# A two-block transformer on one core: smaller gate pieces, a regrouped linear-attention branch, and turned branches evicted by another engine

## The reference

```
x = layer_norm(a*x + 0.5*swiglu(x, w1[0], w3[0], w2[0]))
mix = token_mixing(x)
x = layer_norm(a*x + mix)
x = layer_norm(a*x + 0.5*swiglu(x, w1[1], w3[1], w2[1]))
x = layer_norm(a*x + sigmoid(x @ ple_w_gate) * (p @ ple_w_proj))
```

```
h_rw, h_gla, h_gdn, h_gate = split(x @ w_in)
branches = stack(rwkv7(h_rw), gla(h_gla), gated_deltanet(h_gdn))   # 3 x 256 x 512
merged = sum(sigmoid(h_gate) * (branches @ w_branch))              # 3 x 256 x 1024, summed
return merged @ w_o
```

```
o = att @ v_c + (q_c * exp(b_c)) @ S
S = S * exp(b_end) + (k_c * exp(b_end - b_c)).T @ v_c
return rms_norm(o, norm_g) * silu(gate)
```

## Time and profile before

| | |
|---|---|
| median of 3 runs | 3145.26 us (3143.68 to 3149.9) |
| the profiled execution | 3148.42 us, its span 3146.6 us |
| TensorE busy | 2995.2 us (95%) |
| VectorE, ScalarE, GpSimd busy | 1777.4 us (56%), 694.2 us (22%), 43.8 us (1%) |
| mean granted TensorE clock | 0.986 of full speed |
| HBM read | 425.71 MB, 136 GB/s over the span |

### The profile page before, as it was taken

How to read it: one execution, slowest core, us unless ns; L and a number is a source line. 1 busy time by engine, 2 the same in 40 slices (tenths; PEclk the granted TensorE clock), 3 DMA queues, 4 the chain that set the end, 5 groups by cost and what they waited for, 6 DMA issues and landing times. The chain is left out here.

```text
span 3146.6 us, 52837 instructions
## 1 busy us (share of the span) xinstructions
PE 2995.2 (95%) x22782; PEld 2365.6 (75%) x22782; DVE 1777.4 (56%) x2647; ACT 694.2 (22%) x1326; POOL 43.8 (1%) x83
## 2 busy tenths in 40 slices
PE   8999998999999999999889999989999999998998
PEld 8987764559976998675467995655888887765897
DVE  5554555556556564454565565584433664486665
ACT  2102113212112101212312113282111011254210
POOL 1000000000000000000000000000000000000000
PEclk9999999999999999999999999999999999998999
DMA  8745312227655756322215744101222443231543
GB/s 283 235 162 177 134 47 104 81 81 231 215 187 184 240 186 208 132 75 93 96 55 198 259 165 151 63 19 54 81 81 81 140 154 114 91 124 61 161 161 107
DMA packets 279816, 430.17 MB, mean 137 GB/s; under 512 B 10008, under 2 KB 147712, under 8 KB 279584
## 3 DMA queue, kind: packets, MB, share of 16 engines
q1 hardware_dynamic: 273936, 411.52, 38.7%
q0 software_dynamic: 5024, 14.08, 1.5%
q10 hardware_dynamic: 624, 1.19, 0.1%
HBM read 425.71 MB, written 1.05 MB: 136 GB/s over the span
## 5 line engine op out<-in xcount | busy, mean ns | idle before, releaser
L461 PE MATMUL bank<-arena 64*64 64x64 f32 (+9 forms) x7292 | 748.4, 283 | 43.0 <-DVEq L2376 6.5
L461 PEld LDWEIGHTS bank<-arena 128*128 128x128 f32 (+4 forms) x7292 | 645.7, 163 | 144.0 <-issue 35.3
L461 PE MATMUL bank<-xT,ring 128*128 128x128 f32 (+2 forms) x4512 | 725.1, 320 | 10.3 <-DVE arena L843 5.7
L461 PEld LDWEIGHTS bank<-xT,ring 128*128 128x128 f32 (+1 forms) x4512 | 657.6, 191 | 71.1 <-issue 10.4
L461 PE MATMUL bank<-ring,xT 128*128 128x512 f32 (+2 forms) x1536 | 578.3, 548 | 4.2 <-DVEq L1087 2.0
L461 PE MATMUL bank<-ring,arena 128*128 128x256 f32 (+1 forms) x1584 | 446.6, 434 | 17.5 <-DVE arena L900 6.5
L461 PEld LDWEIGHTS bank<-ring,xT 128*128 128x128 f32 (+1 forms) x1536 | 256.8, 183 | 267.7 <-issue 248.8
L461 PEld LDWEIGHTS bank<-ring,arena 128*128 128x128 f32 x1584 | 301.7, 192 | 134.8 <-issue 87.1
L843 DVE TENSOR_TENSOR arena<-arena,bank 128x256 f32<-128x256 f32 (+1 forms) x198 | 92.2, 466 | 395.8 <-PE bank L461 255.0
L754 ACT COPY arena<-bank 128x256 f32<-128x256 f32 (+1 forms) x264 | 107.6, 408 | 747.5 <-PE bank L461 746.0
L803 DVE TENSOR_TENSOR arena<-ring,arena 128x1024 f32<-128x1024 f32 (+1 forms) x216 | 257.1, 1191 | 7.4
(11 more groups left out here) (413 smaller groups left out, 2149.2 us busy)
## 6 DMA issues: line engine op xcount, KB each, us to landing
ring<-in_ffn_w SPq DMA_DIRECT2D x88, 1024.0 KB, 7.9
ring<-in_w_in SPq DMA_DIRECT2D x32, 2048.0 KB, 7.8
ring<-in_ffn_w_in SPq DMA_DIRECT2D x44, 1024.0 KB, 6.7
arena<-in_ada_w SPq DMA_DIRECT2D x20, 2048.0 KB, 13.4
ring<-in_ffn_w SPq DMA_DIRECT2D x16, 2048.0 KB, 7.9
ring<-in_ffn_w_out SPq DMA_DIRECT2D x12, 2048.0 KB, 7.9
ring<-in_hgrn_w_in SPq DMA_DIRECT2D x12, 2048.0 KB, 7.8
ring<-in_ffn_w SPq DMA_DIRECT2D x8, 1536.0 KB, 6.9
```

The costliest lines, as they stand in the source:

```text
L461: return self.e.matmul(o, lhsT, rhs, start=start, stop=stop, skip_group_check=True)
```

## The change

1. **Gate unit in pieces.** The unit (1,1) of the first branch leaves its place ahead of the solve; its 512 columns become four pieces of 128, at levels 1, 3, 4 and 5 of the solve, each eight products of 128x128 in a bank of its own with a sigmoid of its own on ScalarE.
2. **Second branch by tiles.** The three state products come first and into three places; VectorE makes the three states; then a tile's two chunks are read out into one bank, copied and normalized at once. Late gate steps are shared out anew, and the gate (0,1) is only copied between the levels and goes through its sigmoid later.
3. **Branch turns** go to a `to_act` bank and are evicted by ScalarE; in the second and third branch the head norm's gain is that eviction's scale, so the gain multiply and `normg` are gone.
4. **Epsilons** (and the 1/n of head norms) are bias and scale of the square root; the variance steps on VectorE are gone. Three columns of `small` hold the epsilons.
5. **Norms by halves.** A normalized tile is written in two halves with a signal each. At a feed-forward's end the sum of product 4 stands in the wait for the first tile's root; the modulation product's copy comes after the sixth turn's eviction instead of the eighth. HGRN's readout is normalized and gated by halves.

The core of the diff:

```diff
@@ act_rwkv, act_solve_pair, pe_solve_pair
-            act_gate(act, 1, 1, False, False)
...
+        SOLVE_PIECES = (1, 3, 4, 5)
...
+                    if tt and l in SOLVE_PIECES:
+                        i = SOLVE_PIECES.index(l)
+                        act.wait_ge(to_act.filled, to_act.next_filled())
+                        bank = to_act.filled_bank()
+                        piece = gate_at(1, 1)[:, i // 2, P * (i % 2):P * (i % 2) + P]
+                        ins = act.e.activation(piece, bank[:, 0:P], ACT.Sigmoid)
...
             for l in range(1, last + 1):
                 masked_product(0, l)
                 if l > 1:
                     U_product(1, l - 1)
+                if l in SOLVE_PIECES:
+                    i = SOLVE_PIECES.index(l)
+                    bank = free_bank(to_act)
+                    for k in range(KT):
+                        mm = pe.mm(bank[:, 0:P], x_lhs(k, 1), gate_block[:, k, i * P:(i + 1) * P], k == 0, k == KT - 1)
+                    mm.then_inc(to_act.filled, 1)
                 masked_product(1, l)
@@ pe_gla
-            STEPS = (3, 2, 2, 2, 2, 2, 3)
+            STEPS = (3, 2, 2, 2, 2, 1, 0, 1, 0, 3)
...
+            for n in range(3):
+                tt, c = n // 2, n % 2
...
+                    mm = pe.mm(bank[64 * par:64 * par + 64, hp * P:(hp + 1) * P], gktok[:, tt, h * 64:(h + 1) * 64],
+                               gv_own[tt][c][:, h * P:(h + 1) * P])
+                mm.then_inc(to_dve.filled, 1)
+            late_steps(len(LEVELS) + 1)
             for tt in range(2):
...
+                pe.wait_ge(state_ready, pe.due(state_ready, 2))
...
+                        mm = pe.mm(o, gatt[:, par, 2 * tt + hp], gv_own[tt][c][:, h * P:(h + 1) * P], True, n == 0)
...
+                            mm = pe.mm(o, gQb[:, par, o0:o0 + 64], gS[:, n - 1, hp], False, True)
+                mm.then_inc(to_dve.filled, 1)
+                late_steps(len(LEVELS) + 2 + tt)
@@ dve_gla
+            for n in range(3):
...
+                for hp in range(2) if n else ():
+                    e = hp * SEQ + C * n + C - 1
+                    ins = v.scalar_tensor_tensor(out=gS[:, n, hp], in0=gS[:, n - 1, hp], scalar=gE[:, e:e + 1],
+                                                 in1=bank[:, hp * P:(hp + 1) * P], op0=ALU.mult, op1=ALU.add)
...
+            for tt in range(2):
...
+                v.tensor_copy(br_tok[:, tt], bank[:]).then_inc(to_dve.freed, dve.up(to_dve.freed))
+                dve.wait_ge(to_dve.freed, dve.sent(to_dve.freed))
+                dve_norm_gate(dve, tt, gla_gate[:, tt], gtmp2)
@@ act_branch_turned (new), in place of dve_branch_turned
+            for c in range(2 if by_chunk else 1):
...
+                if gain is None:
+                    ins = act.e.copy(brT[:, :, t0:t0 + n], src)
+                else:
+                    ins = act.e.activation(brT[:, :, t0:t0 + n], src, ACT.Identity, scale=gain)
@@ act_head_std
-            ins = act.e.activation(small[:, 24:32], small[:, 16:24], ACT.Sqrt)
+            ins = act.e.activation(small[:, 24 + first:24 + first + heads], small[:, 16 + first:16 + first + heads], ACT.Sqrt,
+                                   bias=eps, scale=1.0 / n)
@@ dve_normalize
-            ins = v.tensor_scalar(small[:, 2:3], small[:, 1:2], LN_EPS, None, ALU.add)
-            ins.then_inc(var_ready, dve.up(var_ready))
             dve.wait_ge(var_ready, dve.sent(var_ready))
+            if meanwhile:
+                meanwhile()
             dve.wait_ge(std_ready, dve.due(std_ready))
...
-            ins = v.tensor_scalar(x, x, small[:, 0:1], small[:, 4:5], ALU.subtract, ALU.mult)
+            for q in range(2):
+                half = x[:, 512 * q:512 * q + 512]
+                ins = v.tensor_scalar(half, half, small[:, 0:1], small[:, 4:5], ALU.subtract, ALU.mult)
+                ins.then_inc(x_ready, dve.up(x_ready))
@@ dve_ffn7
-                apply(s, half % 2, 0, w.sum[:, 0].rearrange("p (a n) -> p a n", a=2), True)
-                dve.wait_ge(down_products, 7 * h + 6)
-                add(w.sum[:, 1, 0:256], w.u, acc[4])
+                if half % 2:
+                    apply(s, 1, 0, rows0, True, sum_4)
```

More of the change, by code:

```diff
@@ L1040, in dve_scale_x, with act_std @@
             dve.wait_ge(dve_step, dve.sent(dve_step))
-        def act_std(act, n=2):
+        def act_std(act, n=2, rms=False):
+            var, eps = (small[:, 2:3], EPS_RMS) if rms else (small[:, 1:2], EPS_LN)
             for _ in range(n):
                 act.wait_ge(var_ready, act.due(var_ready))
-                act.e.activation(small[:, 3:4], small[:, 2:3], ACT.Sqrt).then_inc(std_ready, act.up(std_ready))
+                act.e.activation(small[:, 3:4], var, ACT.Sqrt, bias=eps).then_inc(std_ready, act.up(std_ready))
                 act.wait_ge(std_ready, act.sent(std_ready))
@@ L1052, in act_prepare_sqrt, with act_ln_turn @@
             act.wait_ge(act_step, act.sent(act_step))
-        def act_ln_turn(act, l, n, tt, qs, between=None):
+        def act_ln_turn(act, l, n, tt, qs, between=None, product=False, home=False):
             for q in qs:
@@ L1063, in act_ln_turn @@
                     done = to_act.freed if k == 3 else act_step
-                    ins.then_inc(done, act.up(done))
+                    ins.then_inc(done, act.up(done, 2 if product and q and k == 3 else 1))
                     act.wait_ge(done, act.sent(done))
@@ L1067, in act_ln_turn @@
                         between()
+                    if product and q and k == 1:
+                        act_ada_product(act, home, act_step)
             act.sem_inc(x_turned, act.up(x_turned))
@@ L1208, in pool_mix @@
             row(GKB, a["gla_gk_b"][l])
+            row(GLAG, a["gla_norm_g"][l])
+            row(GDNG, a["gdn_norm_g"][l])
             e.dma_start(rows[CONV:CONV + 48, :], a["gdn_conv_w"][l].rearrange("i (r p) -> (i r) p", p=P)
@@ L1454, in dve_branch @@
                         dve.wait_ge(dve_step, dve.sent(dve_step))
-                    if tt == 0 and half == (n == 0):
-                        dve_branch_turned(dve, 1, n == 2)
                 if n == 2:
@@ L2269, in act_gla @@
                 act.wait_ge(decay_ready, act.sent(decay_ready))
-                late_unit(l)
-            for _ in range(2):
-                act_head_std(act)
+                if l == 3:
+                    act.wait_ge(to_act.filled, to_act.next_filled())
+                    bank = to_act.filled_bank()
+                    ins = act.e.copy(gate_at(0, 1), bank[:].rearrange("p (a b) -> p a b", a=2))
+                    ins.then_inc(to_act.freed, act.up(to_act.freed))
+                    act.wait_ge(to_act.freed, act.sent(to_act.freed))
+            act_prepare_sqrt(act)
+            act_head_std(act)
+            act.e.activation(gate_at(0, 1), gate_at(0, 1), ACT.Sigmoid).then_inc(act_step, act.up(act_step))
+            act.wait_ge(act_step, act.sent(act_step))
+            act_gate(act, 1, 1)
+            act_prepare_sqrt(act)
+            act_branch_turned(act, 0, cols[:, GLAG:GLAG + 1])
+            act_head_std(act)
+            act_branch_turned(act, 1, cols[:, GLAG:GLAG + 1])
         def dve_gla(dve):
@@ L2390, in dve_branch_gate, with dve_norm_gate @@
             dve.wait_ge(branch_ready, dve.sent(branch_ready))
-        def dve_norm_gate(dve, tt, which, gate, tmp):
-            dve_head_std(dve, head_view(tt), tmp.rearrange("p (h n) -> p h n", h=4), 4, P, HEAD_EPS)
-            dve_branch_gate(dve, tt, which, gate)
+        def dve_norm_gate(dve, tt, gate, tmp):
+            dve_head_std(dve, head_view(tt), tmp.rearrange("p (h n) -> p h n", h=4), 4)
+            dve_branch_gate(dve, tt, gate)
         def pe_gla(pe):
@@ new lines, in pe_gla @@
+            for n in range(3):
+                tt, c = n // 2, n % 2
+                pe.wait_ge(to_dve.freed, to_dve.next_free())
+                bank = to_dve.free_bank()
+                for h in range(4):
+                    hp, par = h // 2, h % 2
+                    mm = pe.mm(bank[64 * par:64 * par + 64, hp * P:(hp + 1) * P], gktok[:, tt, h * 64:(h + 1) * 64],
+                               gv_own[tt][c][:, h * P:(h + 1) * P])
+                mm.then_inc(to_dve.filled, 1)
+            late_steps(len(LEVELS) + 1)
@@ L3182, in act_norm_std @@
                     act.wait_ge(var_ready, act.due(var_ready))
-                    act.e.activation(small[:, 3:4], small[:, 2:3], ACT.Sqrt).then_inc(std_ready, act.up(std_ready))
+                    ins = act.e.activation(small[:, 3:4], small[:, 2:3], ACT.Sqrt, bias=EPS_RMS)
+                    ins.then_inc(std_ready, act.up(std_ready))
                     act.wait_ge(std_ready, act.sent(std_ready))
@@ L3292, in apply @@
                     if half and norm:
-                        dve_norm_tile(dve, s, tt, norm)
+                        dve_norm_tile(dve, s, tt, norm, meanwhile)
+                    elif meanwhile:
+                        meanwhile()
                     if final and half == 0:
```

(8 more changed lines are left out.)

283 lines of the change are left out of this document (120 added, 163 removed).

## The result

| | before | after |
|---|---|---|
| median | 3146.7 us (4 runs, 3143.68 to 3149.9) | 3119.9 us (4 runs, 3114.14 to 3127.2) |
| ratio, 95% interval | | 0.9918 [0.9906, 0.993] |
| profiled execution, its span | 3148.42, 3146.6 us | 3114.14, 3112.4 us |
| TensorE busy | 2995.2 us | 2980.6 us |
| time at granted clock 0.5 (1.2 GHz), within the span | 85.2 us | 66.7 us |

The kernel became 26.8 us faster, 0.8%; the forecast was 3122.5 us, a gain of 22.8. The profiled execution of after is the fastest of its runs. Its span is 34.2 us shorter; 18.5 us less at 1.2 GHz are worth 9.2 of them at most, so 25 us or more are left for the edits themselves.

The account below looks back on a forecast made before the run. TensorE, busy 95% of the span, was taken as the bound, with gains in its gaps. Terms summed to 22.8 us off the profiled 3148.42: 3125.6, or 3122.5 as a median; range 3106 to 3141.

Parts of the forecast that it names:

- pieces in the solve: First branch: four gate pieces among the solve's products shrink its gaps; 4.1 us or 2.4 per layer, 6.5 for both.
- turn 1 of the first branch, product to product: First branch's end: ScalarE evicts turn 1 with nothing ahead, so the next product starts earlier; 1.9 us for both layers.
- second branch, from there to its product: Second branch: table-load wait and state/readout alternation go, its product starts 3.9 us earlier per layer; 7.8 for both.
- third branch: Third branch's end: turn 0's later eviction and tile 1's shorter norm balance; 0 us, -0.75 to 0.3 per layer.
- four layer ends: Layer-end norms: no epsilon step, half writes and the moved sum bring turns earlier; 1.07 us each, 4.3 in all.
- other norms, end: Two other norms 0.6 us each, last mixer's readout norm 0.75, kernel end 2 x 0.15; 2.3 in all.
- The bound in which the pieces do not overlap: Solve: a record costs up to 0.277 us, -6.0 per layer; as rival, 0.20 a record gives 3133 us, chance 0.17.
- three state products of 8 records, 0.1 each: Second branch: state records priced at 0.1 us each from the row of 24 in 2.40, ending at 540.45.
- what is late next: Second branch: ScalarE's table load ahead of turn 0's eviction then delays the branch product, a gap of 2.1 us.
- The two cancel: Third branch: product 0.75 us later by turn 0's eviction, offset by tile 1's shorter norm giving turn 1 early input.
- turn gaps at layer ends under 0.6: Layer ends: sign that the forecast is right, TensorE's gaps ahead of turns falling below 0.6 us.
- The clock did come back: Rival: 1.2 GHz stretches vanish in the solve and behind the second branch's turn; gain 29.3 us, 3116, chance 0.20.

Follow-up runs that it names:

- readout experiment: Changed kernel with the second branch's readouts written chunk by chunk, all four heads of one chunk before the next: 3126.67 us, 0.9937 of the kernel before.
- kept gates: Changed kernel with both late gates of the second branch only copied, their sigmoids after the second root: 3115.15 us, 0.9899 of the kernel before.
- moved step: Kernel with kept gates, plus the late gate step behind the second branch's state products put ahead of the last level pair: 3111.51 us, 0.9886 of the kernel before.
- early table: Kernel with kept gates, plus the third branch's silu table loaded right after its first root by a dummy activation: 3111.21 us, 0.9883 of the kernel before.

## Why the prediction was right

The time fell inside the range, near its middle, and the places and waits that it named are those that changed. That single terms agree in their sums is partly luck. By terms, from starts in the two profiles (before minus after):

| term | forecast | measured, first and second layer |
|---|---|---|
| pieces in the solve | 6.5 | 2.4 and 4.2 |
| turn 1 of the first branch, product to product | 1.9 | 1.5 and 1.8, of the latter 1.7 by the clock |
| second branch, from there to its product | 7.8 | 6.7 and 5.4 |
| third branch | 0 | product 0.9 later, turn 1 on time |
| four layer ends | 4.3 | 2.1 (of it 1.4 by the clock) and 1.2; 0.5 and 0.4 |
| other norms, end | 2.3 | 0.9, 0.6, 0.8 and 0.4 |

These are 28.9 of the 34.2 us between the two spans; the rest is slow stretches that lie elsewhere, as on the second branch's product in the first layer (6.61 before, 3.67 now).

- **Solve.** The mechanism was right; the sum agrees because two misses cancel. The working gave 4.1 per layer without a slow stretch and 2.4 with one, and I took one of each. The slow stretch has gone in both, so the working gives 8.2, and the measured gain is 6.6. The term that was mis-sized is the idle time left, 3.2: it is 5.2 and 3.9. The piece was priced at 2.19 us and takes 2.05, of which the switch between tile shapes is the small part. My gaps were 1.25, 0.65 and 0.37; the first two are 1.09 and 0.52, and in levels 2 to 5 stand gaps of up to 1.4 that I had at 0.37 in all, most of them ended by nothing that the trace names. These are why the solve takes 34.8 to 36.3 us in the nine profiles with pieces: without its gaps it is 30.9 to 31.2 in all of them. The bound in which the pieces do not overlap was far off: a record is 0.128 (2.05/16).
- **Second branch.** The mechanism was right, the size was not. The levels came out to the step: pair 5 and pair 6 at 525.84 and 528.51 are the forecast 534.7 and 537.4 moved by the 8.86 us already won. The step that failed is "three state products of 8 records, 0.1 each" and the readouts priced from the same row: I took a mean over the row of 24 in 2.40 as the price of each record. Of that row 8 go alternately to two halves and 16 to one; its single records already show 0.055 for the first kind and 0.109 for the second. Measured, the 24 state records take 1.46 and the 56 readout records 3.64, where I had 2.4 and 5.6: 2.9 per layer too much. The readout experiment shows the cause for the readouts: the order side by side is worth 1.5 us. The second layer won less since a slow stretch follows its last pair. What the copy in place of the sigmoid and the grouping by tiles are worth one by one is read from the gaps that went; neither was undone alone.
- **ScalarE ahead of the branch product.** Named as what is late next, with 2.1 us (2.3 by its own steps, 550.7 to 553.0); it is 2.66, since the last gate ends 0.2 behind the turn (538.83 against 538.63) and some 0.1 us stands between the steps that follow. The kept gates show the load and the dummy as its cause. The drain of about 1.38 us that the Trainium skill (ScalarE: Activation LUTs, What ACT_TABLE_LOAD costs) adds to a load's 1.28 is not seen in the trace on either side: the load at 538.93 starts 0.10 behind the gate's end, and the dummy starts 0.02 behind the load's.
- **Third branch.** "The two cancel" is true against the kernel before, but not for the reason given: with VectorE's eviction turn 1 finds its norm in time as well. The move itself costs 0.8 us per layer.
- **Turns and norms.** In the second layer the first branch won 0.1 where 0.4 was forecast, beside the slow stretch. At the layer ends the sum holds only with the 1.4 of a slow stretch. The two turns come 0.4 and then 0.9 us earlier in all, near the forecast 1.07, but the new gap of 0.84 ahead of the second modulation product takes 0.4 of it back: the third end, where neither profile has a slow stretch, keeps 0.5. The sign "turn gaps at layer ends under 0.6" did not come; they are 0.97 and 1.12. The half writes, to which I gave 0.4 of each 0.6, win nothing at the layer ends and 0.3 at two other norms. The moved sum and the missing epsilon step are what is left; neither was tried alone.
- **Rivals.** The clock did come back in part: in the solve the slow stretch has gone in all 18 places of the nine profiles with pieces. At the second branch's last pair and the third branch's product there are new ones, so the sign of being wrong "granted clock 0.5 in new stretches" came as well. In the balance it is at most 9.2 of the 34.2 us between the two profiles. New ring waits did not appear (1.0 us of TensorE's idle time ends with a ring transfer, 1.2 before), and no gap ahead of a branch product of the changed kernel was longer than 2.66.

The best kernel here, the changed one with kept gates, moved step and early table, is 40 us faster than the one before on the same chip (3105.4 against 3145.6), and by the ratios about 15 us faster than the changed kernel.

## What to carry over

- Work that fills waits should be cut to the size of the waits and spread over them: the same gate unit gained 0.65 us at most as one block at the first gap, and 2 to 4 us more per layer in four pieces.
- Moving an eviction to an idle engine pays only if that engine has nothing of its own ahead of it; look for its table loads and put activations of other tables behind the eviction.
- The price of a short matrix record depends on where its neighbours write: take it from records whose outputs alternate in the same way, not from the mean of a row.

## What the hardware showed that I had not expected

- The same 56 records of 128x64 by 128x128 take 3.64 us when successive outputs lie in different halves of the partitions, and 5.11 us when four heads in a row write one half. Single records start 0.055 us apart on average where the halves alternate and 0.109 within one half.
- A slow stretch of TensorE follows one and the same place in some executions and not in others. At three places it came in 38 of 48 where the gap was 1.98 to 2.72 us and in none of 20 where it was 0.92 to 1.27; at a fourth it came in all 24 with a gap of 0.91. Time at 1.2 GHz was 54.4 to 90.3 us over the profiles.
